# Two more modulation batches of the first stage on TensorE, eight of their twelve chunks beside the token mix

## The reference, cut to what matters

```
c_act = silu(c)
mod = c_act @ ada_w[0] + ada_b[0]                 # 1 x 6144, six slices of 1024
sh1, sc1, g1, sh2, sc2, g2 = split(mod, 6)
h = rms_norm(x, norm_g[0, 0]) * (1 + sc1) + sh1
u, v = split(gelu(h @ w_in), 2)                   # w_in 1024 x 2048
v = layer_norm(v, ln_g, ln_b)
mixed = einsum('gts,bcsgd->bctgd', tril(w_s), v) + b_s    # 8 groups, token by token
y = (u * mixed) @ w_out                           # w_out 1024 x 1024
x = x + g1 * rms_norm(y, norm_g[0, 1])
h = rms_norm(x, norm_g[0, 2]) * (1 + sc2) + sh2   # and on to the feed-forward part
```

## Time and profile before

| | us |
|---|---|
| median of 3 runs | 1235.71 (1235.05 to 1283.55) |
| the profiled execution | 1238.28 |
| its span in the trace | 1236.5 |
| PE busy | 1111.1 (90%) |
| DVE busy | 850.4 (69%) |
| ACT busy | 535.8 (43%) |

### The profile page before, as it was taken

The page is one execution under the profiler, slowest core; times in us unless marked ns, Lnnn a source line. Parts: engine busy times, 40 slices in busy tenths (PEclk is TensorE's granted clock), DMA queues, the critical chain, the costliest instruction groups (busy, mean ns, idle before and its releaser), DMA issues.

```text
span 1236.5 us, 17498 instructions
## 1 busy us (share of the span) xinstructions
PE 1111.1 (90%) x7050; PEld 943.7 (76%) x7050; DVE 850.4 (69%) x1412; ACT 535.8 (43%) x780; POOL 51.0 (4%) x74
## 2 busy tenths in 40 slices
PE   4694899999989978887899999989998798999997
PEld 1694679988969875554697878869996567999995
DVE  1688487777868854776594478865256658888886
ACT  1532354444454334554353433444552345545453
POOL 0010000000000000000000000030032300000000
PEclk9797989999999976996999999999898799999999
DMA  8992648878848980003375789942431225556510
GB/s 345 359 402 101 238 164 299 305 282 319 292 141 222 357 313 1 1 1 103 102 276 204 305 332 350 318 139 70 137 137 35 100 79 196 186 189 204 172 68 34
DMA packets 129676, 243.55 MB, mean 197 GB/s; under 512 B 6248, under 2 KB 101051, under 8 KB 122427
## 3 DMA queue, kind: packets, MB, share of 16 engines
q1 hardware_dynamic: 125328, 238.81, 55.0%
q10 hardware_dynamic: 4267, 3.62, 1.2%
HBM read 239.27 MB, written 1.05 MB: 194 GB/s over the span
## 4 chain that ended last, share of the span: by engine, by line
PE 73%; DVE 12%; DMA 5%; ACT 4%; issue 4%; POOL 1%; ACTq 1%; SPq 0%; DVEq 0%; POOLq 0%
PE bank L1630 21%; PE bank L1555 10%; PE bank L1557 10%; PE bank L1556 10%; DVE wlo L950 2%; DMA raw<-in_a_w_in_dram 2%; PE bank L1637 2%; DVE tmp L1029 1%; PE bank L1532 1%; PE bank L1792 1%; DMA raw<-in_b_w_in_dram 1%; DVE acc_wide L982 1%; PE bank L1486 1%; DMA vrow<-in_b_ada_dram 1%; PE bank L1807 1%
## 5 line engine op out<-in xcount | busy, mean ns | idle before, releaser
L950 DVE TENSOR_TENSOR wlo<-raw,whi 128x2048 fp32r<-128x2048 f32 (+1 forms) x145 | 329.0, 2273 | 163.0 <-ACT whi L567 162.1
L567 ACT ACTIVATE whi<-raw 128x2048 fp32r<-128x2048 f32 (+1 forms) x145 | 274.5, 1896 | 211.6 <-PE bank L1630 89.3
L1555 PE MATMUL bank<-hcat,whi 128*128 128x256 f32 x1096 | 314.1, 287 | 2.8 <-DVE wlo L950 2.8
L1557 PE MATMUL bank<-hcat,wlo 128*128 128x256 f32 x1096 | 311.7, 284 | 0.0
L1556 PE MATMUL bank<-hcat,whi 128*128 128x256 f32 x1096 | 311.6, 284 | 0.0
L1555 PEld LDWEIGHTS bank<-hcat,whi 128*128 128x128 f32 x1096 | 211.9, 193 | 14.0 <-issue 9.2
L1556 PEld LDWEIGHTS bank<-hcat,whi 128*128 128x128 f32 x1096 | 211.9, 193 | 1.4
L1557 PEld LDWEIGHTS bank<-hcat,wlo 128*128 128x128 f32 x1096 | 211.9, 193 | 0.0
L1444 DVE SCALAR_TENSOR_TENSOR cvt<-ut,vec,cvt 128x189 f32<-128x189 f32 (+2 forms) x176 | 68.2, 429 | 24.2 <-ACT cvt L917 21.8
L982 DVE SCALAR_TENSOR_TENSOR acc_wide<-raw,csil,acc_wide 128x2048 f32<-128x2048 f32 x35 | 82.8, 2365 | 1.3
L1630 PE MATMUL bank<-whi,fhi 128*128 128x512 f32 x240 | 77.5, 404 | 0.0
(11 more groups left out here) (365 smaller groups left out, 1878.9 us busy)
## 6 DMA issues: line engine op xcount, KB each, us to landing
raw<-in_ada_w_dram SPq DMA_DIRECT2D x48, 1024.0 KB, 8.6
raw<-in_ff_w_in_dram SPq DMA_DIRECT2D x32, 1024.0 KB, 6.7
raw<-in_ff_w_out_dram SPq DMA_DIRECT2D x32, 1024.0 KB, 6.8
raw<-in_w_ada_dram SPq DMA_DIRECT2D x24, 1024.0 KB, 8.0
raw<-in_w_up_dram SPq DMA_DIRECT2D x22, 1024.0 KB, 5.1
raw<-in_w_in_dram SPq DMA_DIRECT2D x12, 1024.0 KB, 5.3
raw<-in_w_down_dram SPq DMA_DIRECT2D x11, 1024.0 KB, 5.0
raw<-in_a_w_in_dram SPq DMA_DIRECT2D x8, 1024.0 KB, 10.6
```

The lines of the kernel that those rows point to most:

```text
L567: act.activation(whi[:, m % SPL, 0:w], raw[:, pl.nm[m] % RAW, 0:w], ACT.Copy).then_inc(s_hi, 1)
L950: dve.tensor_tensor(wlo[:, m % SPL, 0:w], raw[:, pl.nm[m] % RAW, 0:w], whi[:, m % SPL, 0:w], ALU.subtract).then_inc(s_lo, 1)
L1555: pe.matmul(dst, wh[:, kt, n], ah[:, kt, :], start=kt == 0, stop=False)
L1557: mm = pe.matmul(dst, wl[:, kt, n], ah[:, kt, :], start=False, stop=kt == KT - 1)
```

## The change

G0A and S0B join the batches that PE multiplies. Their twelve chunks leave DVE and go into PE's list: one each ahead of V2, V3, U0 and U1 (batch G0A), four behind `open_y`, two behind AO0 and two behind AO1 (batch S0B). The order of the loads changes to fit: U2 and U3 come before the first chunks of S0B. The column step of G0A moves to between U2 and U3, its row copy on ACT to behind the second gelu of U, and `mods(G0A)` with `gain_diag` on DVE to ahead of the layer norm's last part. As bank 7 is now held by the sums of S0B, the mix's last quarter goes to bank 4 once DVE has read the first quarter from it, and comes on PE behind the four chunks. The high parts of AO1 and AO2 come on ACT behind the last gelu.

```
-    PE_BATCHES = (S0, S2, G2B)
+    PE_BATCHES = (S0, G0A, S0B, S2, G2B)
...
-            ada_loads([0, 0, 1, 1, 1, 1, 2, 2, 2, 2, 0, 0][j])
+            ada_loads([0, 0, 1, 1, 1, 1, 0, 0, 4, 2, 2, 0][j])
... on ACT, in the loop over U
-                    splits(m + 4)
+                    splits(min(m + 4, M_AO[0] + 1))
...
-                    if j == 2:
+                    if j == 1:
                         ada_row(G0A)
+                splits(M_AO[2] + 1)
... on DVE
+                mods(G0A)
+                gain_diag(U_GMLP, G_N1)
                 dve.wait_ge(s_lr, 1)
...
-                mods(G0A)
-                gain_diag(U_GMLP, G_N1)
...
-                                           ps[4 + b][:, :]...
+                                           ps[4 + b % 3][:, :]...
... on PE
                 for j in range(4):
+                    if j >= 2:
+                        ada_chunks(1)
                     linear_mid(M_V[j], hh, hl, tm=True, o=0 if j == 0 else None)
...
                 for j in range(4):
+                    if j < 2:
+                        ada_chunks(1)
                     linear_mid(M_U[j], hh, hl)
                     if j == 2:
-                        ada_sum(G0A)
-                ada_cols(G0A)
+                        ada_cols(G0A)
...
-                ada_bank_free(G0A + 1)
-                for b in range(4):
...
+                for b in range(3):
+                    mix(b)
+                pe.wait_ge(s_wTc, 2)
                 open_y()
+                ada_chunks(4)
                 for j in range(4):
                     pe.wait_ge(s_oa, j + 1)
+                    if j == 0:
+                        mix(3)
                     if j == 3:
                         gain_row(U_GMLP, 0)
                         gain_row(U_GMLP, 1)
-                        ada_sum(S0B)
                     rows_onto_y(M_AO[j], *h_rows(2 * j), last=j == 3).then_inc(s_mm, 1)
+                    if j < 2:
+                        ada_chunks(2)
                 ada_cols(S0B)
```

More of the change, by code:

```diff
@@ L1148, in _ @@
                     link(dve.tensor_tensor(t32[:, q, :].rearrange("p g (a t) -> p g a t", a=2),
-                                           ps[4 + b][:, :].rearrange("p (g a t) -> p g a t", g=2, a=2), bias, ALU.add))
+                                           ps[4 + b % 3][:, :].rearrange("p (g a t) -> p g a t", g=2, a=2), bias, ALU.add))
                     link(dve.tensor_tensor(h32[:, q, :], t32[:, q, :], u_fm[:, q, :], ALU.mult))
@@ L1707, in _, with mix @@
                 for j in range(4):
+                    if j < 2:
+                        ada_chunks(1)
                     linear_mid(M_U[j], hh, hl)
                     if j == 2:
-                        ada_sum(G0A)
-                ada_cols(G0A)
+                        ada_cols(G0A)
+                def mix(b):
+                    for g in (2 * b, 2 * b + 1):
+                        for tt in range(2):
+                            c0 = (g % 2) * T + tt * P
+                            mm = pe.matmul(ps[4 + b % 3][:, c0:c0 + P], v_tm[:, tt, g * P:g * P + P], wT[:, g, :], start=True, stop=True)
+                    mm.then_inc(s_mix, 1)
                 pe.wait_ge(s_wT, 1)
```

## The result

Over 20 runs of each kernel the changed one takes 1238.13 us in the median, the kernel before 1234.36 us. The ratio is 1.0026 with a 95% interval of 1.0014 to 1.0039: 3.2 us slower (1.7 to 4.8), which many runs tell from no change and which is far inside 2%. The profiled execution's span is 1238.2 us against 1236.5.

The account below looks back on a forecast made before the run. PE was taken to bound the V and U products, then a chain of waits from the mix to AO3. Terms summed to +1.1 to +3.6 us, middle +2.3: 1235.71 + 2.3 = 1238.0 us, eight-in-ten range 1232.5 to 1242.5.

Parts of the forecast that it names:

- Chunk price, 0.97 us: On PE between products: each chunk takes 0.97 us at full clock, twice that at half; four cost 3.9 us.
- The sum that leaves: On PE ahead of U2: the sum of G0A's accumulator goes away, saving 1.0 us.
- The stall for the row copy, 1.4 us: PE, done with U2, waits 1.4 us for G0A's row copy on ACT, behind AO0's high part and load.
- The mix at 104.2, released by the norm: After U3: the mix waits for DVE's layer norm and starts at 104.2 instead of 101.31, +2.9 us.
- The clock at the mix, left open: Before the mix: PE idles 3.1 us; whether its clock then stays full or falls was left undecided.
- case (b): Half clock from the mix: epilogue +2.9 us, last quarter 1.6 us late for DVE, AO0 at 120.5, total +3.6 us.
- the two cases: From the mix on: at full clock AO0 starts at 118.0, total +1.1 us; at half clock 120.5, total +3.6 us.
- 4.8 us of multiply-adds off the path, 3.9 us of chunks onto it: Around AO0: S0B's DVE multiply-adds ahead of it go, 4.8 us; four PE chunks behind AO0 and AO1 add 3.9 us.
- AO3, -1.5 to +1.5 us: At AO3: a shifted clock phase could change its 3 us at half clock to 0 or 6, -1.5 to +1.5 us.
- Rival 2 (relief in full): DVE's relief around AO0 shows in full: -0.9 us at the least, -4.8 if chunks hide, 1231 to 1235; chance 0.13.
- rival 3: Shorter PE idling before AO0 keeps the clock up; AO0's cold start costs 2.6 us less, 1235.4; chance 0.12.
- Rival 4 (the ring): Late loads through the ring leave PE waiting for AO1 and falling to half clock, 1242.3; chance 0.10.

Follow-up runs that it names:

- Experiment 1: Changed kernel with G0A's row copy on ACT moved ahead of AO0's high part; ratio to the kernel before 0.9995.
- Experiment 2: Changed kernel with `mods(G0A)` and `gain_diag` on DVE put back behind the layer norm's last part; ratio to the kernel before 0.9997.
- experiment 5: Changed kernel with 20 matmuls of zeros added on PE behind the mix's last quarter; ratio to the kernel before 1.0007.
- experiment 6: Kernel before with only G0A's four chunks on PE, ahead of V2, V3, U0, U1, old orders and load order; ratio to the kernel before 1.0089.
- experiment 4: Changed kernel with the two chunks behind AO0 moved ahead of it; ratio to the kernel before 0.9983.
- the changed kernel with AO3 early: Changed kernel with AO3's high part on ACT ahead of the two copies of the gate rows; ratio to the kernel before 0.9992.
- experiment 7: Changed kernel with only S0B on PE, G0A's chunks back on DVE and its partition sum behind U1; ratio to the kernel before 0.9988.
- experiment 8: Changed kernel, row copy before AO0's high part, `mods(G0A)` and `gain_diag` behind the norm, two chunks before AO0, last two behind gate rows; ratio to kernel before 0.9917.
- experiment 9: AO3's high part ahead of the gate rows' copies, in three kernels: on experiment 8 0.9901, kernel before 0.9979, changed kernel 0.9992, all against the kernel before.
- experiment 10: "and AO3 early" with last chunks behind AO3, S0B's row copy behind y's squares, one feed-forward weight split before the update; ratio to the kernel before 0.9902.
- and AO3 early: Kernel of experiment 8 with AO3's high part on ACT ahead of the gate rows' copies; ratio to the kernel before 0.9901.

## Why the prediction was right

The time lies 0.1 us from the forecast of 1238.0. That closeness is chance: the level of the kernel before turned out 1.35 us lower over 20 runs than over three, and the loss larger, 3.8 us between the medians (3.2 by the ratio) instead of 2.3. What the steps say counts for more. Their clock times agree in part by luck too: V0 ended 1.2 us sooner in this profile than in the one that they were counted from.

- **Chunk price, 0.97 us: too low among products.** From the start of a chunk to the start of the next product it is the forecast's 1.0 us for one, 1.85 for a pair and 3.57 for four. But the records on either side of the seam lie further apart too (0.21 and 0.23 us instead of 0.12), and the forecast's reading of the earlier trace rows left that out. By the gelus a single chunk costs 1.18 us. A pair costs 2.1 us: AO1 to AO2 start 136.61 - 129.05 = 7.56 us apart, and a product alone takes 5.44 us (before, 56 matmuls at full clock took 139.75 - 127.03 us, so 24 take this). The sum that leaves was worth 1.18 us as well. So ahead of U2 it is 3.5 us instead of 2.9, and among AO0 to AO2 4.2 instead of 3.9.
- **The stall for the row copy, 1.4 us: held**, 1.55 us. AO0's high part began at 91.61 (91.9 forecast), the row copy at 93.43, the column step at 94.06 (94.4). Experiment 1 shows that it is this order that costs it.
- **The mix at 104.2, released by the norm: the path held, the size did not quite.** It starts at 103.96, released by `v_tm`, but counted from V0 that is 3.8 us later than before and not 2.9; most of the difference is the price of the chunks. Experiment 2 shows it: with the mods behind the norm U3's gelu releases it, with 0.78 us idle.
- **The clock at the mix, left open: half of case (b).** It fell at 103.9, and AO0 started at 119.02, between the two cases. The epilogue began 2.6 us late, as (b) has it (106.14 against 103.50), but the last quarter came only 0.25 us after DVE wanted it, not 1.6: the clock was back at 107.3, sooner than I took from the earlier trace rows.
- **4.8 us of multiply-adds off the path, 3.9 us of chunks onto it: held.** AO0 to the gate rows took 23.4 us against 19.07; the 4.3 us more are the two pairs of chunks, and the start at half clock was as long as before (5.4 us against 5.2).
- **AO3, -1.5 to +1.5 us: held**, at the far end: 148.91 to the column step at 157.36, 8.45 us against 7.16, so +1.3.
- **In sum** the stage, counted from V0, lost 3.6 us to the gate rows and 4.9 us to AO3's end. That is the upper end of the forecast (+3.6, and up to 1.5 for AO3), not its middle of 2.3. The runs say 3.2 us.
- **Rival 2 (relief in full) and rival 3 (AO0 at full clock) didn't happen.** The price in rival 3, 2.6 us, was right: 2.5 in experiment 5.
- **Rival 4 (the ring) was the right mechanism in the wrong place.** AO1 and AO2 came in time in the changed kernel. With the old load order such a wait costs far more than I gave it, 11 us (experiment 6). I had weighed the reorder of the loads only by where it put AO0.

## What to carry to other kernels

When work that frees a ring's slots moves to another engine, the slots are freed at that engine's pace and in its order: look at what the load queue holds behind them before counting the engine time won. Put moved work where its new engine waits, not where there is a seam between products: the same twelve chunks were worth 3.2 us lost or, with four of them moved into idle stretches and two orders turned round, 10 us gained. And an instruction that only waits for a load must not stand ahead of one that another engine is waiting for.

## What the runs showed of the hardware

The same idle stretch ahead of the mix left the clock at full or not: 3.00 us ended at the lower level (0.94 from 103 to 104 us, then 0.50), 2.98 us in experiment 1 at full (all 24 records of the mix in 2.92 us). What PE did before differs. In the four kernels in which the clock fell there (changed, experiments 4 and 5, and the changed kernel with AO3 early) PE had also waited 1.3 to 1.6 us for the row copy some ten us earlier; in the two in which it stayed up (experiments 1 and 7) it had waited 0.24 us or not at all. That this is the cause isn't shown.

Ahead of AO0 the clock fell in experiment 4 within 2.7 us of idling, and after the 0.7 us in experiment 5 it was up. In experiments 8, 9 and 10 PE idled 2.7 to 3.1 us there and AO0 began at full clock; the level fell 0.5 to 0.8 us into it (in the kernel "and AO3 early" it is 1.00 up to 115.00 and 0.50 from 115.25, with AO0 from 114.39). The time at half clock afterwards was 3.4 us at the mix of the changed kernel and 6.4 us at that of the kernel before, counted from its column step. So a forecast for a stretch of about 3 us can only give both cases. The Trainium skill (TensorE: Matmul & The Clock Gate, "What's actually happening") says that the level follows how busy the array has been recently; experiment 5 agrees, where nothing but matmuls of zeros ahead of AO0 made it 2.5 us faster.
